# Each expert's output combined by itself, over four row tiles of 32 partitions

## The reference, cut to what matters

```
x = x + attention_0(norm(x)); x = x + moe_0(norm(x))      # 16 heads, causal stick-breaking
x = x + attention_1(norm(x)); x = x + moe_1(norm(x))      # window of 128, shared K/V, sinks
out = norm(x) * final_norm

moe(z): a router picks one of 4 groups, and 2 of its 8 experts, for each token
  for g in 4 groups, e in 8 experts:
     h = silu(z @ w_gate[g, e]) * (z @ w_up[g, e])        # 1024 -> 512
     y = y + share[token, g, e] * (h @ w_down[g, e])      # 512 -> 1024, share is 0 for most tokens
```

## Time and profile before

| | |
|---|---|
| median of 3 runs | 1128.93 us (1127.11 to 1131.37) |
| the profiled execution, own time | 1130.43 us |
| its span | 1128.6 us |
| PE busy | 866.7 us, 77% |
| ACT busy | 234.0 us, 21% |
| DVE busy | 177.5 us, 16% |
| DMA | 432.80 MB, mean 383 GB/s over the span |
| granted TensorE clock, mean | 0.914 |

### The profile page before, as it was taken

How to read it: one execution, slowest core, us unless ns; L and a number is a source line. 1 busy time by engine, 2 the same in 40 slices (tenths; PEclk the granted TensorE clock), 3 DMA queues, 4 the chain that set the end, 5 groups by cost and what they waited for, 6 DMA issues and landing times.

```text
span 1128.6 us, 18471 instructions
## 1 busy us (share of the span) xinstructions
PE 866.7 (77%) x7850; PEld 482.1 (43%) x7850; DVE 177.5 (16%) x486; ACT 234.0 (21%) x545; POOL 17.9 (2%) x38
## 2 busy tenths in 40 slices
PE   8999998886657656775669999888567766686656
PEld 4688554453224323442335555445223432253223
DVE  1023231111001100110003523111000110011001
ACT  2066523121001200120002333213000210021001
POOL 0000000000000000000001100000000000000000
PEclk9999999998889988998899999999888987798878
DMA  9972278999999999999999945999999999999996
GB/s 377 429 300 76 82 291 330 427 429 428 428 429 428 428 429 429 428 430 428 427 427 427 425 163 206 410 428 428 429 428 429 429 429 430 428 428 428 428 427 264
DMA packets 31278, 432.80 MB, mean 383 GB/s; under 512 B 3472, under 2 KB 3728, under 8 KB 4880
## 3 DMA queue, kind: packets, MB, share of 16 engines
q1 hardware_dynamic: 31248, 432.38, 91.0%
HBM read 431.31 MB, written 1.05 MB: 383 GB/s over the span
## 4 chain that ended last, share of the span: by engine, by line
DMA 36%; PE 33%; SPq 25%; ACT 2%; DVE 2%; issue 2%; DVEq 0%; POOL 0%; POOLq 0%; ACTq 0%
DMA ring<-in_w_moe 35%; SPq L452 25%; PE ps L1306 6%; PE ps L1173 5%; PE ps L1158 5%; PE ps L1356 3%; PE ps L1133 2%; PE ps L1380 2%; PE ps L1294 2%; PE ps L1282 2%; PE ps L1253 1%; PE ps L1406 1%; PE ps L1443 1%; PE ps L1113 1%; PE ps L1214 1%
## 5 line engine op out<-in xcount | busy, mean ns | idle before, releaser
L1306 PE MATMUL ps<-ring,xT 128*32 128x256 f32 x4096 | 288.7, 434 | 145.6 <-DMA ring<-in_w_moe 135.4
L1306 PEld LDWEIGHTS ps<-ring,xT 128*32 128x32 f32 x4096 | 136.4, 122 | 288.4 <-DMA ring<-in_w_moe 177.4
L1356 PE MATMUL ps<-ring,hT 128*32 128x256 f32 x2048 | 147.6, 437 | 49.0 <-DMA ring<-in_w_moe 36.5
L1356 PEld LDWEIGHTS ps<-ring,hT 128*32 128x32 f32 x2048 | 73.6, 122 | 104.6 <-issue 57.4
L671 ACT ACTIVATE sil<-ps 128x128 f32<-128x128 f32 x64 | 17.7, 277 | 379.2 <-PE ps L1306 379.2
L965 DVE COPY oT<-ps 32x256 f32<-32x256 f32 x128 | 53.3, 417 | 265.1 <-PE ps L1356 264.2
L678 ACT ACTIVATE oT<-ps 32x256 f32<-32x256 f32 x128 | 48.1, 376 | 196.5 <-PE ps L1356 195.7
L960 DVE TENSOR_TENSOR sil<-sil,ps 128x128 f32<-128x128 f32 x64 | 18.4, 287 | 399.7 <-ACT sil L671 399.7
L1282 PE MATMUL ps<-oT 128*128 128x512 f32 x128 | 60.6, 617 | 8.5 <-DVE oT L965 8.5
L1294 PE MATMUL ps<-oT,h 128*128 128x256 f32 x256 | 58.9, 383 | 1.5 <-DVE oT L945 1.5
L1158 PE MATMUL ps<-ring,oT 128*128 128x512 f32 x128 | 56.9, 597 | 0.0
(11 more groups left out here) (148 smaller groups left out, 518.5 us busy)
## 6 DMA issues: line engine op xcount, KB each, us to landing
ring<-in_w_moe SPq DMA_DIRECT2D x192, 2048.0 KB, 49.1
ring<-in_w_a SPq DMA_DIRECT2D x7, 2048.0 KB, 27.5
ring<-in_w_b SPq DMA_DIRECT2D x4, 2048.0 KB, 41.9
ring<-in_w_a SPq DMA_DIRECT2D x2, 1024.0 KB, 8.9
h<-in_x SPq DMA_DIRECT2D x2, 512.0 KB, 4.6
ring<-in_w_b SPq DMA_DIRECT2D x1, 1024.0 KB, 41.9
out<-h SPq DMA_DIRECT2D x4, 256.0 KB, 2.1
ring<-in_final_norm SPq DMA_DIRECT2D x1, 512.0 KB, 39.8
```

The costliest lines, as they stand in the source:

```text
L1306: last = MM(ps[CAP * j:CAP * (j + 1), B_GU, 0:2 * P].rearrange("p (u f) -> p u f", u=2), xg[:, kk, CAP * e:CAP * (e + 1)], w[:, :, k, P * ...
L1356: last = MM(ps[CAP * c:CAP * (c + 1), B_Y, 0:256], hT[:, b, CAP * j:CAP * (j + 1)], w[:, j, 256 * c:256 * (c + 1)], start=j == 0, stop=j = ...
```

## The change

`yq` becomes 128 x 256: one expert alone, its four quarters of the width in the four quarters of the partitions, just as they stand in `B_Y`. So a single ScalarE copy of 128 x 256 brings it over, and VectorE's copies go. `combine(it, e)` runs for every expert: eight matmuls, each with 32 rows of contraction (quarter `c` of the partitions), 128 columns and 256 wide, quarter `c` going to PSUM bank `c`. Row tile t = 0 takes the first half of every bank and t = 1 the second, which changes the layout of `acc`. It runs one expert late, after `gate_up(e, 1)` of the next expert, and for expert 7 at the end of the group. The shares of an expert must now stand in every quarter of the partitions: `transpose_shares` runs four times a group, for two experts each, as 16 matmuls with the identity in four column tiles, and ScalarE copies the result four times. As both row tiles share the banks, one semaphore counts the sums of both, the transposes after the first layer go to banks 4 to 7, the small routing tensors move up in their buffer, and VectorE's final scaling waits for both squares. `start_sums` makes four matmuls of 256 in place of two of 512 for each row tile. The identity matmuls of `keep_warm` write to bank `B_HT`.

```diff
-        acc = ps[:, 0:4, :].rearrange("p (t h) n -> p t h n", t=T)
+        acc = ps[:, 0:4, :].rearrange("p c (t n) -> p t c n", t=T)
...
-                        if e == 1:
-                            act.wait_ge(selt_psum, it + 1)
-                            nc.scalar.activation(selT.rearrange("p q t n -> p (q t n)"), ps[:, B_SEL, :],
+                        if e % 2:
+                            act.wait_ge(selt_psum, it * (NE // 2) + (e // 2 + 1))
+                            nc.scalar.activation(selT.rearrange("p x t n -> p (x t n)"), ps[:, B_SEL, :],
                                                  ACT.Copy).then_inc(selt_done, 1)
...
-                        r0 = CAP * (e % QUAD)
-                        for c in (2, 3):
-                            last = nc.scalar.activation(
-                                yq[r0:r0 + CAP, 256 * c:256 * (c + 1)],
-                                ps[CAP * c:CAP * (c + 1), B_Y, 0:256], ACT.Copy)
-                        last.then_inc(y_act, 1)
+                        nc.scalar.activation(yq, ps[:, B_Y, 0:D // 4], ACT.Copy).then_inc(y_act, 1)
...
-                        dve.wait_ge(y_psum, it * NE + (e + 1))
-                        r0 = CAP * (e % QUAD)
-                        for c in (0, 1):
-                            last = V.tensor_copy(yq[r0:r0 + CAP, 256 * c:256 * (c + 1)],
-                                                 ps[CAP * c:CAP * (c + 1), B_Y, 0:256])
-                        last.then_inc(y_dve, 1)
...
                 dve.wait_ge(rstd_done, T * 4 + t + 1)
+                if t == 0:
+                    dve.wait_ge(squared, T * 4 + T)
...
-                def combine(it, q):
-
-                    pe.wait_ge(y_act, it * NE + (QUAD * (q + 1) + 1))
-                    pe.wait_ge(y_dve, it * NE + (QUAD * (q + 1) + 1))
-                    if q == 0:
-                        pe.wait_ge(selt_done, it + 1)
-                    for i in range(4):
-                        t, half = i // 2, i % 2
-                        MM(acc[:, t, half, :], selT[:, q, t, :], yq[:, 512 * half:512 * (half + 1)],
-                           start=False, stop=False, skip_group_check=True).then_inc(summed[t], 1)
+                def combine(it, e):
+
+                    pe.wait_ge(selt_done, it * (NE // 2) + (e // 2 + 1))
+                    pe.wait_ge(y_act, it * NE + (e + 2))
+                    for t in range(T):
+                        for c in range(4):
+                            r = slice(CAP * c, CAP * (c + 1))
+                            last = MM(acc[:, t, c, :], selT[r, e % 2, t, :], yq[r, :], start=False,
+                                      stop=False, skip_group_check=True)
+                    last.then_inc(summed, 1)
...
-                        for q in range(2):
+                        for x in range(2):
                             for t in range(T):
-                                last = nc.tensor.transpose(ps[:, B_SEL, P * (2 * q + t):P * (2 * q + t + 1)],
-                                                           selg[:, t, P * q:P * (q + 1)], ident)
+                                at = P * (T * x + t)
+                                for c in range(4):
+                                    last = MM(ps[CAP * c:CAP * (c + 1), B_SEL, at:at + P],
+                                              selg[:, t, CAP * (e0 + x):CAP * (e0 + x + 1)], ident,
+                                              start=True, stop=True, skip_group_check=True)
...
-                        if e == QUAD:
-                            combine(it, 0)
+                        if e:
+                            combine(it, e - 1)
...
-                    combine(it, 1)
+                    combine(it, NE - 1)
```

More of the change, by code:

```diff
@@ L257, in build @@
         cut = cutter(flat_o, KD * SEQ)
-        yq = cut(D)
         selg = cut(T * NE * CAP).rearrange("p (t n) -> p t n", t=T)
-        selT = cut(2 * T * P).rearrange("p (q t n) -> p q t n", q=2, t=T)
-        tiny = cutter(flat_o, D)
+        selT = cut(2 * T * P).rearrange("p (x t n) -> p x t n", x=2, t=T)
+        yq = cut(D // 4)
+        tiny = cutter(flat_o[:, D:2 * D], D)
         logit = tiny(T * NLOG).rearrange("p (t n) -> p t n", t=T)
@@ L362, in build @@
         y_act = sem("y_act")
-        y_dve = sem("y_dve")
-        summed = [sem(f"summed{t}") for t in range(T)]
+        summed = sem("summed")
         added = [sem(f"added{t}") for t in range(T)]
@@ L397, in wait_m, with quarters, xt_bank @@
                 eng.wait_ge(landed[b], its * (16 * PER[0][b]) + lit * (16 * PER[1][b]) + here)
+        def quarters(rows, t, half):
+            return rows[:, t, D // 2 * half:D // 2 * (half + 1)].rearrange("p (c n) -> p c n", c=2)
+        def xt_bank(n, t):
+            return 2 * t + (4 if n == 2 else 0)
         def rows_stand(eng, n, t):
@@ L406, in rows_stand, with sums_stand @@
                 eng.wait_ge(added[t], 2)
-        def sums_stand(eng, t, its):
-            eng.wait_ge(summed[t], its * 4)
+        def sums_stand(eng, its):
+            eng.wait_ge(summed, its * NE)
         def passes(eng, layer, before, group, peel=False):
@@ L581, in square @@
                 rows = h[:, t, :]
+                unread = (v_rows[:, t, :], after_attention, q_rows[:, t, :], after_attention,
+                          flat_x[:, t, :])[n]
                 if n == 4:
-                    sums_stand(act, t, its)
-                    rows = acc[:, t, :, :].rearrange("p h n -> p (h n)")
+                    sums_stand(act, its)
+                    rows = acc[:, t, :, :]
+                    unread = unread.rearrange("p (c n) -> p c n", c=4)
                 else:
@@ L689, in _ @@
             for t in range(T):
-                sums_stand(act, t, its)
-                nc.scalar.activation(h[:, t, 0:D // 2], acc[:, t, 0, :], ACT.Copy).then_inc(added[t], 1)
+                sums_stand(act, its)
+                nc.scalar.activation(quarters(h, t, 0), acc[:, t, 0:2, :], ACT.Copy).then_inc(added[t], 1)
             for t in range(T):
@@ L975, in _ @@
             for t in range(T):
-                sums_stand(dve, t, its)
-                V.tensor_copy(h[:, t, D // 2:D], acc[:, t, 1, :]).then_inc(added[t], 1)
+                sums_stand(dve, its)
+                V.tensor_copy(quarters(h, t, 1), acc[:, t, 2:4, :]).then_inc(added[t], 1)
             store_transposed(2, [(2, xTkv), (3, xT)])
@@ L1112, in transpose_rows @@
                     for k in range(KD):
-                        last = nc.tensor.transpose(ps[:, 2 * t + k // 4, P * (k % 4):P * (k % 4 + 1)],
+                        last = nc.tensor.transpose(ps[:, xt_bank(n, t) + k // 4, P * (k % 4):P * (k % 4 + 1)],
                                                    src[:, t, P * k:P * (k + 1)], ident)
@@ L1257, in start_sums @@
                 def start_sums(t):
-                    for half in range(2):
-                        MM(acc[:, t, half, :], ident, h[:, t, D // 2 * half:D // 2 * (half + 1)], start=True,
+                    for c in range(4):
+                        MM(acc[:, t, c, :], ident, h[:, t, D // 4 * c:D // 4 * (c + 1)], start=t == 0,
                            stop=False, skip_group_check=True)
@@ L1335, in group @@
                         b = e % 2
[L1336 to L1337 removed]
+                        if e % 2:
+                            transpose_shares(e - 1)
                         if e:
```

22 lines of the change are left out of this document (9 added, 13 removed).

## The result

The changed kernel takes 1138.61 us (median of 5 runs, 1137.53 to 1139.27), the kernel before, run beside it, 1131.37 us (5 runs, 1127.11 to 1131.63). The ratio is 1.0075, with a 95% interval of 1.0060 to 1.0089 (it is taken over all runs; the two medians alone would give 1.0064): slower by 0.75%. The forecast was 1129.7 us with a range of 1124 to 1137, so the result lies outside it, on the slow side. The profiled execution took 1139.18 us with a span of 1137.4 us, 8.8 us more than the span before.

The account below looks back on a forecast made before the run. It took the expert weights' stream (DMA always busy, 73% of the span) as the bound, plus TensorE's path at the layer ends. Terms -1.9 - 0.9 + 3.6 = +0.8 us on 1128.93 gave 1129.7 us, range 1124 to 1137.

Parts of the forecast that it names:

- the price of the fetches: In both expert streams: 55 more instruction fetches, each 1.04 us of one engine, spread over 16 engines, +3.6 us in all.
- Fetches bind: Rival: fetches fall on few DMA engines, or TensorE stalls at layer ends; four engines 1140 us, one 1183; chance 0.08.
- The combination: Each expert's 16 records in four row tiles run together: 1.0 us, or 1.2 where something waits for the end.
- pairs: Rival: row tiles overlap only two at a time, 2.1 us a combination, 1134.1 us; chance 0.08 shared with loads in a row.
- one after another: Rival: a combination's row tiles do not overlap, 3.7 us each, 1140.5 us with the fetches; chance 0.07.
- Costs nothing: In the streams: TensorE's 3.6 us more work per group is free, as it is busy 72 of 103 us.
- the upper prices: In the streams: combinations at 3.7 and shares at 3.6 us, 36 us more a group, would only just reach the transfers' pace.
- Expert 6's combination in expert 7's way: At both ends: it stands between expert 7's last gate/up and the transpose, which comes 0.35 us later.
- End of layer 0: Chain to the transposes: +0.35 expert 6, -0.50 copy, -2.47 combination, +0.75 copy into `h` no longer hidden; sum -1.9 us.
- End of the kernel: After the last expert: -2.6 us at the combination's end, +1.75 for squares and scaling; sum -0.9 us.
- The rival that decides by row tiles: At both ends: row tiles not running together, deciding from about 2.2 us a combination; 1140.5 us one after another, chance 0.07.
- The loop stays: Rival: the longer loop stays on the chip, so no fetches in later passes; 1126.1 us, chance 0.22.

Follow-up runs that it names:

- pad34: The kernel before with 34 tiny unused matmuls for each of experts 0 to 6 in its loop, about 2,670 instructions a pass; 1145.89 us, ratio 1.0135.
- pad5: The kernel before with 5 tiny unused matmuls for each of experts 0 to 6, 1,860 instructions a pass; 1136.72 us, one run.
- dup: The changed kernel with shares repeated by VectorE and turned by four full transposes, 1,975 instructions a pass; 1137.51 us, ratio 1.0060.
- pad9: The kernel before with 9 tiny unused matmuls for each of experts 0 to 6, 1,971 instructions a pass; 1140.75 us, ratio 1.0096.
- pad17: The kernel before with 17 tiny unused matmuls for each of experts 0 to 6, about 2,200 instructions a pass; 1142.85 us, ratio 1.0103.
- lean: The changed kernel without combinations of experts 0 to 5, shares turned for expert 7 only (sums incomplete), 1,774 instructions a pass; 1130.43 us, ratio 0.9997.
- pad3: The kernel before with 3 tiny unused matmuls for each of experts 0 to 6, 1,804 instructions a pass; 1131.35 us, one run.
- split3: The changed kernel as split2, but with no identity matmuls in expert 7, 862 records a pass; 1131.86 us, ratio 1.0015.
- split2: The changed kernel as split, but experts 4 to 6 combined ahead of both gate/up halves of expert 7, replacing identity matmuls; 1130.58 us, ratio 1.0006.
- split: The changed kernel with experts 0-3 and 4-6 combined wide, the latter between expert 7's gate/up halves, only expert 7 in row tiles; 1137.56 us, ratio 1.0069.
- its two shifted copies: lean with 64 or 128 empty instructions ahead of TensorE's first work; 1131.57 and 1130.06 us, one run each.

## Why the prediction was wrong

**The step that failed** is the price of the fetches: "Spread over 16 engines that is 0.065 us of the stream, 3.6 us in all". That they would happen was right. There were 66 more of them, not 55; that alone would make the 3.6 us 4.3. But they cost 6.0 us in each layer, 12.0 in all. With 12.0 in place of 3.6 the sum is -1.9 - 0.9 + 12.0 = +9.2 us; with the ends as they were measured it is -2.2 - 1.2 + 12.0 = +8.6, and the span grew by 8.8. The mechanism at both ends was right; the term of the streams was too small by more than three.

Two things are in the 12.0. A weight load is cut over the 16 DMA engines and is complete when the last of them has landed its part. These are the 16 landings of one load near 567 us in the order in which they came, in us after the first:

```
before  0.00 0.26 0.32 0.38 0.41 0.57 0.64 0.77 1.08 1.24 1.61 1.71 2.02 2.12 2.33 2.51
after   0.00 0.19 0.39 0.83 0.93 1.10 1.14 1.94 6.39 6.56 6.57 6.93 7.94 8.08 8.27 8.71
pad34   0.00 0.17 0.55 0.57 0.76 1.02 1.40 1.78 8.04 8.29 8.48 8.56 9.48 9.75 9.76 9.81
```

Eight engines are where they were; the other eight are over 4 us behind. So the fetches fall on half of the engines. I had called this possible for four engines or for one ("Fetches bind", chance 0.08, 1140 us for four) and passed over eight, although nothing in the trace had said 16: that the first pass's six fetches "did not lower the rate visibly" could not tell 16 from 8.

The second thing is the size. This is the sum of the 16 lags of a load, and the last lag, in us, at three times (heads of the columns) in each layer:

```
           239.7        415.7        533.2    |  737-742      913-918      1031-1036  us
before   15.1, 2.44   16.4, 2.51   16.5, 2.50 | 11.9, 2.17   14.8, 2.16   13.8, 2.08
after    19.2, 2.38   42.9, 5.52   59.5, 8.70 | 11.7, 2.00   38.7, 5.15   54.4, 6.75
pad5     16.7, 2.31   40.1, 5.08   54.3, 7.04 | 14.1, 2.42   17.1, 2.41   17.1, 2.41
```

Between 239.7 and 533.2 us the changed kernel's sum of lags grows by 40.3 us, and 25 fetches lie there: 1.6 us of an engine for each, where the packet itself takes 1.07 (the median). Over all the fetches of a layer the growth was 1.55 to 1.70 each in five kernels (this one, dup, pad9, pad17, pad34). By the last gate/up load of layer 0 the lags add up to 67.7 us, where they were 18.1, and 31 fetches more lie ahead of it than before. That is 49.6 us of engine time: 3.1 us of the stream if shared by 16 engines, 6.2 if by 8. The stretch grew by 6.0.

The first part of that load lands at 582.1 us in both kernels. Its last part lands at 584.6 before and at 590.8 now, and there the last gate/up slot begins. The same holds wherever I cut a stream: this is its growth over the kernel before, and the growth of the last lag of its last gate/up load, in us, for layer 0 and layer 1.

| kernel | growth of the streams | growth of the last lag |
|---|---|---|
| changed | 6.0, 6.0 | 6.2, 6.3 |
| dup | 6.5, 6.3 | 6.6, 6.2 |
| pad9 | 5.8, 5.6 | 5.8, 5.7 |
| pad17 | 6.3, 5.9 | 6.5, 6.0 |
| pad34 | 7.5, 7.9 | 7.6, 8.0 |
| pad5 | 5.6, 0.3 | 5.5, 0.4 |
| lean | -0.1, 0.3 | -0.2, 0.4 |

The rate shows only half of it. Between the cuts of layer 0 the weights' queue moved 176.33 MB where it had moved 175.02; at 423 GB/s the 1.3 MB are 3.1 us in which the fast engines ran ahead with loads that were not wanted yet. The other 2.9 us are the lower rate. That is why neither the DMA share (1.00) nor the rate shows the whole loss. Why a fetch costs its engine 0.5 us beyond its packet, no run tells.

The Trainium skill, "Runtime: NRT & Kernel Launch", section "Instruction fetch mechanics", on which I had called the fetches certain, gives TensorE 2048 instructions, filled in blocks of 256, so eight blocks. One copy of pad5's loop was fetched again with about 1,860 a pass, 9% below that. The trace does not contradict the eight blocks: that copy took nine packets a pass, so it seems to lie across nine blocks though it is only 7.3 long; that the copy which stayed lies across eight is argued and not shown. The Trainium skill calls the crossing of a block mostly hidden; for TensorE it was, for the weights it was not.

**Point by point, the rest:**

- *The combination*, 1.0 us and 1.2 with its end: 1.08 and 1.19. The 16 records start four at a time, 7 ns apart; the second four comes 0.32 us after the first, each further four after 0.215 us, where I had 0.23. The weight loads of a four start 7 ns apart too, so loads in a row (1.8 us) did not come, and neither did pairs or one after another. The Trainium skill, "TensorE: Matmul & The Clock Gate", section "The mechanism", says that tiles in different row groups overlap and start about 4 ns apart; the trace agrees with the first and shows 7.
- *The shares*, 0.9 us a call: 0.87 us from a call's start to the next work's, 4.2 us of busy time in four calls a group. Hidden, as forecast.
- *TensorE's load in the streams*: 308.5 us busy of 419.9. "Costs nothing" was right: pad9 and pad17 have the loss without this work. One sum under it was not: at the upper prices 72 + 36 is 108 us, more than the 103 of a group, so that case would have cost some 5 us a group. It did not come.
- *The copy*: from the down projection's end to the combination 0.45 us, where it was 1.02. Forecast -0.50, came -0.57.
- *Expert 6's combination in expert 7's way*: the wait of 0.68 us became 1.08. Forecast +0.35, came +0.4.
- *End of layer 0*: forecast -1.9, came -2.2. *End of the kernel*: forecast -0.9, came -1.2. The new order of squares and scaling, forecast 5.2 us from the last combination on, took 1129.82 to 1134.80, 5.0.
- *"TensorE's own pause for them is hidden by its 30 us of idle time a group"*: right. It stood still for 16.3 us in six passes, up to 3.7 at once, and the streams lost no more by it than pad9's, which has no such wait.
- *The rival that decides by row tiles* is out: a combination took 1.08 us, not 2 to 4. *"Fetches bind"*, with a chance of 0.08, is the rival that came nearest, by its mechanism too: not all engines carry the fetches. Its 1140 us for four engines lies close to 1138.61 by luck, since there are eight and each fetch costs more than its packet. *The loop stays*: out, but lean, the nearest that I have to it, shows no gain, 1130.43 against 1130.24. My 1126.1 for it left out that a shorter end runs into the code that follows the loop.

**What lean and the splits add.** Before, TensorE's sequencer leaves the loop at 593.8 us and wants the code of attention 1 from 599.36 us on, when ScalarE has its operands ready. In lean it leaves at 590.7 and goes on with new code only at 597.1; the 3 us of its earlier end are lost. That the pause is a wait for code rests on the packet in it and on there being no semaphore to wait for; it was not undone by an experiment. Its lengths (2.3 to 2.6 us in pad3, 1.5 in split3, 3.1 in split2, 3.8 in lean, over 5 in split) differ. But its end has a rule: in all seven kernels with such a pause exactly one packet lies by it, and TensorE goes on 2.3 to 2.6 us after that packet starts (594.63 and 597.10 in lean, 597.00 and 599.54 in split, 597.08 and 599.56 in split3), 1.2 to 1.5 us after its 1.1 us are over. So the pause ends with the fetch; why the packet starts when it does stays open. In the changed kernel, whose loop is fetched on every pass, there is no such pause. In the kernel before a packet comes at 597.3 us too, but there TensorE stands still for 0.9 us and waits for ScalarE.

## What to carry to other kernels

A loop's code is a resource of TensorE: count the instructions of one pass (weight loads and waits too) before a change that trades few wide matmuls for many narrow ones, and see by the instruction queue's packets whether the loop still stays on the chip. Under a saturated stream price a small extra transfer by the engine that it falls on, not by the mean over all: the load that is waited for is complete with its last engine, and neither the DMA share nor the rate shows that lag in full. When a loop's end is made shorter, look at what the first instructions after it wait for, code included, and at the clock they then find.

## What the runs showed of the hardware

- A loop with 1,804 TensorE instructions a pass stayed on the chip, with 1,860 it did in one layer's copy and not in the other's (nine packets a pass), with 1,971 in neither.
- Instruction fetches of 16 KB delay the DMA engine that serves them by 1.55 to 1.7 us each, while their packets take 1.07 (median), and fall on about half of the 16 engines. Each added 0.18 to 0.23 us to a saturated stream.
- Four row tiles of 32 with float32 run together: 16 records of 256 columns in 1.08 us.
- After the end of a loop that stayed on the chip, TensorE stood still for 1.5 to 5.4 us within the next 40 instructions or so, in seven kernels (pad3, lean and its two shifted copies, the three splits), and went on 2.3 to 2.6 us after a packet of the instruction queue had started. In lean, where it had been idle for 3.80 us before its next long piece of work, the granted clock was 0.50 for the 6 us that followed, and 32 matmuls took 10.01 us instead of 7.15.
